# The LRU convolution reads a padded copy in SBUF instead of PSUM

## The reference, cut to what matters

```python
def odd_mixer(h, w_in, conv_w, conv_b, w_a, b_a, w_x, b_x, lam, w_out):
    gate, xr = jnp.split(h @ w_in, 2, axis=-1)
    xr = causal_depthwise_conv(xr, conv_w, conv_b)   # 4 taps: output t sees t-3..t
    y = rg_lru(xr, w_a, b_a, w_x, b_x, lam)          # 4 heads of 256 channels
    return (jax.nn.gelu(gate) * y) @ w_out
# rg_lru, per channel: r, i = sigmoid of xr times w_a, w_x (per head); a = exp(-8 r softplus(-lam));
# h_t = a_t h_{t-1} + sqrt(1 - a_t^2) (i_t x_t)
```

## Time and profile before

| | |
|---|---|
| median of 3 runs | 3557.21 us (3554.34 to 3557.93) |
| profiled execution | 3557.93 us, span 3556.2 us |
| mean granted clock of TensorE | 0.982 of full speed |
| TensorE, matmul | 3398.1 us busy, 96% |
| VectorE | 1715.9 us, 48% |
| ScalarE | 759.5 us, 21% |
| GpSimd | 1474.3 us, 41% |

### The profile page before, as it was taken

How to read it: one execution, slowest core, us unless ns; L and a number is a source line. 1 busy time by engine, 2 the same in 40 slices (tenths; PEclk the granted TensorE clock), 3 DMA queues, 4 the chain that set the end, 5 groups by cost and what they waited for, 6 DMA issues and landing times.

```text
span 3556.2 us, 39514 instructions
## 1 busy us (share of the span) xinstructions
PE 3398.1 (96%) x15717; PEld 2778.4 (78%) x15717; DVE 1715.9 (48%) x1805; ACT 759.5 (21%) x1114; POOL 1474.3 (41%) x723
## 2 busy tenths in 40 slices
PE   8999889999999999998999999999899999999998
PEld 6777668788888888887888888887787777767786
DVE  3444334423323257776423323357767666475542
ACT  4333232100000033334100000032112313223111
POOL 3211566334433355355344333355653231413264
PEclk9999989999999999999999999999999999999999
DMA  4110023111111141123111111143224110201133
GB/s 152 46 31 27 18 93 109 48 48 47 47 49 51 47 136 48 42 65 125 48 48 47 48 53 47 47 130 89 69 63 140 36 44 24 68 18 50 36 125 106
DMA packets 244366, 227.94 MB, mean 64 GB/s; under 512 B 8940, under 2 KB 206228, under 8 KB 244264
## 3 DMA queue, kind: packets, MB, share of 16 engines
q1 hardware_dynamic: 224480, 180.32, 17.0%
q10 hardware_dynamic: 19784, 46.22, 3.7%
HBM read 188.65 MB, written 33.64 MB: 63 GB/s over the span
## 4 chain that ended last, share of the span: by engine, by line
PE 78%; DVE 10%; issue 4%; POOL 3%; ACT 3%; ACTq 1%; DMA 0%; DVEq 0%; SPq 0%; POOLq 0%
PE ps L357 25%; PE ps L359 24%; PE ps L358 24%; PE ps L587 1%; PE ps L2445 1%; POOL w_lo L347 1%; PE ps L1032 1%; ACT b_junk L470 1%; DVE Y L712 1%; POOL w_hi L345 1%; ACTq L2049 1%; POOL Y L666 1%; DVE ml_st_lo L2673 1%; DVE ml_st L2669 0%; PE ps L1912 0%
## 5 line engine op out<-in xcount | busy, mean ns | idle before, releaser
L345 POOL TENSOR_TENSOR w_hi<-raw,one_col 128x1024 fp32r<-128x1024 f32 x275 | 542.7, 1974 | 1791.9 <-PE ps L359 1768.3
L357 PE MATMUL ps<-H_hi,w_hi 128*128 128x512 f32 x2720 | 1087.2, 400 | 44.9 <-POOL w_lo L347 7.5
L359 PE MATMUL ps<-H_hi,w_lo 128*128 128x512 f32 x2720 | 1066.4, 392 | 0.0
L358 PE MATMUL ps<-H_lo,w_hi 128*128 128x512 f32 x2720 | 1065.8, 392 | 0.0
L347 POOL TENSOR_TENSOR w_lo<-raw,w_hi 128x1024 fp32r<-128x1024 f32 x275 | 692.6, 2518 | 21.6
L357 PEld LDWEIGHTS ps<-H_hi,w_hi 128*128 128x128 f32 x2720 | 515.2, 189 | 155.6 <-issue 22.8
L359 PEld LDWEIGHTS ps<-H_hi,w_lo 128*128 128x128 f32 x2720 | 514.1, 189 | 108.5
L358 PEld LDWEIGHTS ps<-H_lo,w_hi 128*128 128x128 f32 x2720 | 515.0, 189 | 101.3 <-issue 1.9
L357 PE MATMUL ps<-w_hi,ffn_f_hi 128*128 128x512 f32 x704 | 274.2, 390 | 0.0
L358 PE MATMUL ps<-w_lo,ffn_f_hi 128*128 128x512 f32 x704 | 274.2, 390 | 0.0
L359 PE MATMUL ps<-w_hi,ffn_f_lo 128*128 128x512 f32 x704 | 274.2, 390 | 0.0
(11 more groups left out here) (461 smaller groups left out, 4698.3 us busy)
## 6 DMA issues: line engine op xcount, KB each, us to landing
raw<-in_w_in SPq DMA_DIRECT2D x49, 512.0 KB
raw<-in_ffn_w_gate SPq DMA_DIRECT2D x44, 512.0 KB
raw<-in_ffn_w_up SPq DMA_DIRECT2D x44, 512.0 KB
raw<-in_ffn_w_down SPq DMA_DIRECT2D x44, 512.0 KB
b_X<-x_dram SPq DMA_DIRECT2D x24, 512.0 KB, 5.3
x_dram<-Y SPq DMA_DIRECT2D x24, 512.0 KB, 5.0
raw<-in_ev_w_in SPq DMA_DIRECT2D x17, 512.0 KB
x_dram<-Y ACTq DMA_DIRECT2D x16, 512.0 KB, 3.6
```

Of the source, the lines that this page charges most:

```text
L345: pool.tensor_tensor(w_hi[s][:, :n], raw[s][:, :n], one_col[:, :].broadcast_to([P, n]), ALU.mult).then_inc(split_hi, 1)
L357: pe.matmul(o, l_hi, r_hi, start=first, stop=False)
L358: pe.matmul(o, l_hi, r_lo, start=False, stop=False)
L359: return pe.matmul(o, l_lo, r_hi, start=False, stop=last)
```

## The change

The stage gets a buffer `xpad` of two tiles, each with three zero columns ahead. ScalarE copies each x tile from PSUM into it, in its queue ahead of the rounding. VectorE takes all four taps from it; each older tap is the same 1024 columns wide, begun one column further left. The wait of VectorE is for the copy, and so is TensorE's for the banks 0 and 1. The low part of tile 0 is made right after its convolution, before the one of tile 1. The buffer takes the place of the work tiles T4 and T5, which the recurrence of the second tile uses.

```diff
-        A_, B_, C_ = (T0[:, :], T3[:, :]), (T1[:, :], T4[:, :]), (T2[:, :], T5[:, :])
+        A_, B_, C_ = (T0[:, :], T3[:, :]), (T1[:, :], xpad[:, 0, 3:]), (T2[:, :], xpad[:, 1, 3:])
...
         def act_in(e, j, name, i):
+            for t in range(2):
+                e.wait_ge(multiplied, stream.number(name, t, i))
+                e.activation(xpad[:, t, 3:], pair(t), ACT.Copy).then_inc(s["x_read"], 1)
             for t in range(2):
                 e.wait_ge(s["conv"], 2 * j + t + 1)
                 e.activation(xc_hi[:, t, :], xc[:, t, :], ACT.Copy).then_inc(s["xc_hi"], 1)
...
-        def dve_in(e, o, j, name, i):
+        def dve_in(e, o, j):
             for t in range(2):
-                e.wait_ge(multiplied, stream.number(name, t, i))
-                o(e.tensor_scalar(xc[:, t, :], pair(t), col("od_conv3", 2 * j + t), col("od_conv_b", 2 * j + t), ALU.mult, ALU.add))
+                e.wait_ge(s["x_read"], 2 * j + t + 1)
+                o(e.tensor_scalar(xc[:, t, :], xpad[:, t, 3:], col("od_conv3", 2 * j + t), col("od_conv_b", 2 * j + t), ALU.mult, ALU.add))
                 for back in (1, 2, 3):
-                    ins = e.scalar_tensor_tensor(xc[:, t, back:], pair(t)[:, 0:S - back], col(f"od_conv{3 - back}", 2 * j + t), xc[:, t, back:], ALU.mult, ALU.add)
+                    ins = e.scalar_tensor_tensor(xc[:, t, :], xpad[:, t, 3 - back:3 - back + S], col(f"od_conv{3 - back}", 2 * j + t), xc[:, t, :], ALU.mult, ALU.add)
                     if back < 3:
                         o(ins)
                 ins.then_inc(s["conv"], 1)
-            for t in range(2):
                 e.wait_ge(s["xc_hi"], 2 * j + t + 1)
                 e.tensor_tensor(xc_lo[:, t, :], xc[:, t, :], f32(xc_hi[:, t, :]), ALU.subtract).then_inc(s["xc_ready"], 1)
...
+            o(e.memset(xpad[:, :, 0:3], 0.0))
```

More of the change, by code:

```diff
@@ L1483, in lru @@
     def lru(tmp_free):
-        T4, T5, xc, xc_hi, xc_lo, out_hi, out_lo, G, T0, T1, T2, T3 = carve(
-            ("lru_T4", [P, S], F32), ("lru_T5", [P, S], F32), ("lru_xc", [P, 2, S], F32), ("lru_xc_hi", [P, 2, S], F32R), ("lru_xc_lo", [P, 2, S], F32R),
+        xpad, xc, xc_hi, xc_lo, out_hi, out_lo, G, T0, T1, T2, T3 = carve(
+            ("lru_xpad", [P, 2, 3 + S], F32), ("lru_xc", [P, 2, S], F32), ("lru_xc_hi", [P, 2, S], F32R), ("lru_xc_lo", [P, 2, S], F32R),
             ("lru_out_hi", [P, 2, S], F32R), ("lru_out_lo", [P, 2, S], F32R), ("lru_G", [P, 2, S], F32),
             *[(f"lru_T{n}", [P, S], F32) for n in range(4)])
-        names = ("gate_sq", "gate_arg", "gate_tanh", "conv", "xc_hi", "xc_ready", "gates_read", "decay",
+        names = ("x_read", "gate_sq", "gate_arg", "gate_tanh", "conv", "xc_hi", "xc_ready", "gates_read", "decay",
                  "root", "out_full", "out_hi", "out_ready", "y_added", "down_part", "wax_part")
@@ L1517, in pe_out @@
                     elif n < 2:
-                        e.wait_ge(s["conv"], 2 * (j + 1) + n + 1)
+                        e.wait_ge(s["x_read"], 2 * (j + 1) + n + 1)
                     else:
@@ L1547, in pe_gates @@
                     if c < 2:
-                        e.wait_ge(s["conv"], 2 * j + c + 1)
+                        e.wait_ge(s["x_read"], 2 * j + c + 1)
                     else:
@@ L1699, in dve @@
                 e.wait_ge(w, v)
-            dve_in(e, o, 0, first, 0)
+            o(e.memset(xpad[:, :, 0:3], 0.0))
+            dve_in(e, o, 0)
             dve_chain(e, o, 0)
@@ L1704, in dve @@
                 o.enter(i, IN_STEPS + CHAIN_STEPS)
-                dve_in(e, o, i + 1, loop, i)
+                dve_in(e, o, i + 1)
                 dve_out(e, i, loop, 4, i)
@@ L1708, in dve @@
             o.leave(L - 1)
-            dve_in(e, o, L, end, 0)
+            dve_in(e, o, L)
             dve_chain(e, o, L, lambda a, b: dve_out(e, L - 1, end, 5, 0, a, b))
```

## The result

The changed kernel takes **3578.6 us** (median of 4 runs, 3574.8 to 3580.4) against 3556.2 for the kernel before (4 runs beside it): a ratio of 1.0062, 95% interval 1.0047 to 1.0077, so 22.5 us slower. The forecast was 3572 us with a range of 3563 to 3578, so the result lies 0.6 us above the range. The direction and most of the terms hold; the first head does not.

The account below looks back on a forecast made before the run. TensorE was taken to bound the whole kernel, with VectorE and ScalarE alone setting the last head's chain. Terms 5.5 + 3.6 + 4.4 + 0.4 + 0.8 = 14.7 us on the 3557.21 median gave 3572 us, range 3563 to 3578.

Parts of the forecast that it names:

- the first head: LRU head 0: TensorE's late fourth product chunk covers nearly all lateness, at worst one 1.6 us collision; +0.4 us.
- The verdict of the bound: Whole kernel: TensorE is the bound, without a pause in the LRU stage up to 1590 us; VectorE's lateness counts beyond TensorE's lead.
- Head 1: LRU head 1: second convolution 5.5 us late through copy, blocked taps and order, with TensorE already waiting; +5.5 us.
- Head 2: LRU head 2: second convolution 5.4 us late, less TensorE's lead over VectorE of 1.8; +3.6 us.
- The lead of 1.8 us: LRU head 2: VectorE's first add ends about 1512.1, TensorE takes that bank at 1513.91, so 1.8 us of lateness is covered.
- The alternation of taps and splits: Convolutions from SBUF: VectorE's taps and GpSimd's split operations hold each other in turn; a split pair costs about 1.6 plus 2.1 us.
- Last head: Last LRU head: second convolution 7.5 us late, partly regained on the cubic; gate closes at 1593.4 against 1589.02, +4.4 us.
- The saving on the cubic: Last LRU head: the split of 1579.50 meets the convolution instead of the gate's cubic, so 3.8 us go away.
- Clock: TensorE: new waits in heads 1 and 2 may bring one or two drops to 1.2 GHz; +0.8 us, bounds 0 and 3.
- The largest term: VectorE's taps from SBUF: GpSimd's weight splits can block them, about 1.6 plus 2.1 us per split pair falling fully on them.
- The rival with collisions that spread: Late cubic, close and low parts of heads 1 and 2 meet next splits, or clock drops: 3575 to 3580 us, 15%.
- the signs named ahead: LRU stage: TensorE waits some 5 us in head 1, 3 to 4 in head 2, 8 in the last; stage 13 to 16 longer.

Follow-up runs that it names:

- copies alone: Changed kernel with taps read from PSUM and low parts after both convolutions, leaving only ScalarE's copies and VectorE's wait for them: 3556.3 us, +0.1 us.
- the kernel before with the zeroing first: Kernel before, with GpSimd zeroing Y before it splits the first head's last chunks: 3556.5 us, +0.4 us.
- the one with ScalarE's taps: Kernel before, with the newest tap of each tile made by ScalarE from PSUM and three taps left to VectorE: 3556.0 us, +0.4 us.
- The late zeroing: Changed kernel, with GpSimd's zeroing of Y held back until both convolutions of the first head are over: 3572.7 us, +16.5 us.
- the order alone: Kernel before, taps from PSUM and no copies, with only tile 0's low part moved between the two convolutions: 3563.6 us, +7.4 us.
- the two-input tap: Changed kernel, with each tile's first tap in the two-input form of the other taps, bias spread along the row: 3575.4 us, +19.2 us.
- the low parts at the end: Changed kernel, with both low parts put back after both convolutions: 3566.8 us, +10.7 us.

## Why the prediction was right and where it was wrong

**The verdict of the bound was right.** TensorE had no pause in rows 1 and VectorE's path set what pauses came; the loss arrived at TensorE as waits for VectorE, or for ScalarE behind it (1.99 and 0.74).

**Head 1: +5.5 forecast, +5.45 measured** between output split and second convolution. **Head 2: +3.6 forecast, +3.4 measured** (TensorE's product at 1530.79 is 16.26 late, the one at 1451.06 was 12.83, both less the 0.62). The lead of 1.8 us read from rows 5 and 6 was real. The alternation of taps and splits, taken over from the mLSTM rows, was the right model. That head 1 agrees to 0.05 is luck in part: the split was forecast to hold the first tap, but came 0.59 us after that tap had begun and held the older ones; its first operation ended 3.93 us after the output split instead of 2.95, and the convolution was over 5.84 later instead of 6.74. Two errors of about 0.9 cancelled. One size was off in every head: the first tap takes 0.81 and not 0.69, which is the price without coefficients per channel.

**Last head: +4.4 forecast, +4.1 measured** up to the gate's close (1610.02 against 1589.02 is 21.0; less the 0.62 of the start and the 16.26 brought along, 4.1). The saving on the cubic came as forecast. But the sum ended at the gate's close, and what comes after was taken as unchanged. TensorE stood 7.52 us before the gate products (8 were forecast), and I wrote that this fits into its later waiting. It does for TensorE. It does not for GpSimd, whose next split TensorE releases: that went from 1590.38 to 1617.01, onto an operation of the recurrence, for another **+2.1**. This was not tried alone, but the runs bear it out: between the gate's close and the last output split every kernel in which TensorE stops before the gate products loses 2.1 to 2.3 us, and the three in which it doesn't (copies alone, the kernel before with the zeroing first, and the one with ScalarE's taps) at most 0.2.

**The step that failed is the first head**: "TensorE's fourth product chunk comes late enough to cover nearly all of it, with at worst one collision of 1.6. I take +0.4." It was **+7.4** (the output split is over at 1422.99 against 1414.98). The cover was there, 3.5 us of VectorE's idling for the second gate tile and 4.6 of a cubic that was held before and is not now, but the lateness was 15.2 us, not one collision. I priced a collision by the length of one split operation; the operation in the way was of 6.95 us and stood directly behind the split, so that both counted as one. The late zeroing shows the size: of the 7.0 us missed here it gives back 5.9 in the median and 6.6 in the trace of head 0.

**Clock: +0.8 forecast, no time of its own in the loop, and an open share in the last head.** PEclk went from 1.00 to 0.98 in the first stretch, but the drops of head 0 (0.50 in the 4 us from 1378) and of head 1 lie ahead of VectorE's first add, under its lateness, and after the stop of 2.22 at 1530.79 the sums run on at 1.00. With the order alone the same kind of drop costs 1.6: the term is real, and its place decides. In the last head it has a place that the sum hides: after the stop of 7.52 the gate products run at a granted 0.53 for the 4 us from 1604, and the split at 1617.01 starts 13.11 us after the first of them where it started 11.19 after it before. So 1.9 us of that split's lateness are the clock's, and how much of the +2.1 would be left without them was not tried. 7.4 + 5.45 + 3.4 + 4.1 + 2.1 makes 22.45, all of what was measured; since each term is the growth of one lateness from one point of the stage to the next, the sum has to come out, and it proves none of the causes.

**The parts forecast by name.** The order alone was worth 7.4 where the prediction's prices give 5.4; the copies alone nothing that can be told (1.3 in the profile, at most 2.8 by the interval) where they give some 2 (1.5 less the 0.5 in head 1, 1.35 less the 0.21 in the last). The largest term was rightly named: that GpSimd can block VectorE accounts for 15.3 of 22.5 as long as the order is changed too, 10.6 without. The rival with collisions that spread, 3575 to 3580 at 15%, is the one that came about, by a spread to head 0 and to the recurrence, not to the low parts of heads 1 and 2 that it named. Of the signs named ahead, the stops of TensorE came out otherwise: 2.6 us in head 1 where some 5 were forecast (6.69 had already been spent in head 0), 3.0 in head 2 and 7.5 in the last, and the stage is 22.45 longer, not 13 to 16.

The Trainium skill, "SBUF — State Buffer", section "Who interferes with whom", says that an operation of VectorE with two inputs in SBUF contends with a GpSimd operation that reads SBUF and not with one that only writes, and that one in a two-port mode, which a multiply with scalars can enter, contends with any and blocks, or is blocked, for the whole of an operation. The traces agree on which operations meet: the two-input tap was over 1.08 us after the split operation and 5.8 before the zeroing's end, the taps from PSUM took 1.28 beside any split, and the one-input tap stood until the zeroing's end.

## What to carry to other kernels

Before moving a buffer from PSUM to SBUF, list every operation of GpSimd that lies under its readers, write-only ones and one-time ones like a zeroing included, and shift that list by the lateness that the change itself brings: the collision that costs is the one that wasn't there before. For each fast one-input operation, price a GpSimd operation and the zeroing directly behind it as one long operation. And where TensorE releases GpSimd, a new stop of TensorE moves the splits that come after it, so the sum may end only where both kernels are in step again.

## What the runs showed of the hardware that I had not expected

- A waiting one-input operation of VectorE was kept out through GpSimd's split operation and the zeroing directly behind it: 9.78 us with one zeroing, 10.05 us with one in eight pieces. It did get in where a split operation came next: between the two operations of one split, 0.08 us apart (0.56 us after the first had ended; the low parts at the end, head 0), and between the zeroing and the next split, whose row starts at 1369.20, before the zeroing's end at 1369.24. So a gap in the rows is not what decides; in these traces the boundary that kept it out had a zeroing behind it. Why is not shown.
- The end of a held one-input operation lay 0.54 to 0.56 us behind the end of GpSimd's operation that it got in after, in all twelve traces; that of a two-input one lay 1.08 to 1.09 behind (the earlier trace rows and the two-input tap).
- Stops of TensorE of about 2 us were followed by different granted clocks: 0.77 and 0.80 for 4 us each after 2.21 us (the order alone, 1.6 us lost), 0.86 and 0.71 after 1.99 (the changed kernel, head 1), but 1.00 after 2.22 (the changed kernel, head 2). One of 0.82 in the run with the copies alone left it at 1.00.
- The multiply with a coefficient and a bias per channel takes 0.81 us from SBUF where the one with constants takes 0.69, and 1.34 from PSUM.
